# Router of a mixture-of-experts stage: the low parts of the token rows on GpSimd, the first one-hot matrix without the counts, the last tile's statistics over its own columns

## The chip, the cores and the metric

One Trainium2 chip, one of its cores. The time is that of the device, in microseconds, from the first to the last instruction of the program and what lies around it; of several executions the median is given. Everything is float32; products with large weights are made of three matmuls of values rounded for a faster matmul form (high by high, low by high, high by low).

## The reference

256 tokens (and 16 meta tokens) of width 1024 go through a first block (two layers with four gated feed-forward parts, a chunked linear attention and a sliding-window attention) and then a second one, whose end is where the change lies:

```python
mixed = (sigmoid(gate_a) * y_a + sigmoid(gate_b) * y_b) @ w_out
x = layer_norm(DN_ALPHA * h + mixed, ln1_g, ln1_b)
# hier_moe: 4 groups of 8 experts, hidden 512, top 2 of the chosen group
grp = argmax(x @ w_group + b_group)
top_v, top_i = top_k(e_logits of that group, 2)
weights = softmax(top_v) * p_grp
expert = grp * 8 + top_i                     # 512 assignments
order = argsort(expert); rows of x sorted by expert, each expert's rows padded to a block
y[token] += ((silu(gate) * up) @ w_down[e]) * w   for each block
x = layer_norm(DN_ALPHA * x + y, ln2_g, ln2_b)
```

## The kernel before, in words

The program is written engine by engine, with semaphores set by hand; no scheduler reorders it. Until about 1297 us of the profiled execution it works on dense layers. Then comes `wo`, the last projection (eight tiles of 128 features by 256 tokens, two tiles to a weight unit): VectorE (DVE) adds each tile to `h` (line 2188), and TensorE (PE) turns the tile into token rows (`tokens(m)`, a transposition into the banks `xtok` and a product with the 36 routing columns). `bn_stats` over the token rows (lines 2186 and 2191) gives mean and variance of the layer norm, and ScalarE (ACT) then writes the scaled rows twice, once rounded (`m_xhi`, line 1530) and once as they are (`m_o`, line 1532), four pieces of 128x512, and after each it raises the bank's `evac`.

The router runs on DVE, on 128 partitions of tokens (two halves of 128 tokens, side by side): the best group, the best two experts (`first_max`, line 2223), one-hot marks `o1` and `o2`, and their sum `M0, M1` with `m_ready` (line 2242). PE counts with them: `cnt` is how many assignments each expert has, `pos` the place of each token in its expert (columns 0 to 63) and the same plus 64 times the expert (columns 64 to 127). Tokens are put into blocks of 64 slots; the first 32 blocks are the first 64 rows of each expert, and what an expert has beyond 64 rows goes to further blocks, for which the counts must be summed over the experts (lines 2262 to 2268). From that comes `dest`, and from `dest` the one-hot matrix `m_P` of a quad of four blocks (`choose`, `choose_2`), with which PE gathers the rows: `gather(q, n)`, sixteen matmuls for each half (q = 0, 1 and q = 2, 3), with the rounded rows and with their low parts `m_xlo`, which `rows_low` makes (line 2251, 128x512 each, four of them; the semaphore `rows_lo` counts them).

Then the experts run, four to a quad, nine quads here: `expert(quad, s)` multiplies the 64 gathered rows with 2048 KB pieces of weights, two of `w_gate_up` and one of `w_down`. SyncE's queue (SPq) loads the pieces (line 504) into seven places, and each load waits until PE has begun the piece after the one that it overwrites (`exp_begun`). The first pieces land while the router runs.

To keep PE active it multiplies with zeros while it waits: eight matmuls of 512 columns before `m_ready` (four of them clear the output banks), three after `pos`. GpSimd (POOL) issues a few DMAs, and from the first expert's `silu_made` on it makes `x2` (lines 588 and 590, 128x1024 each), which PE needs in the third expert.

## Time and profile before

| | us |
|---|---|
| median of 3 executions (1826.84 to 1829.95) | 1828.28 |
| the profiled execution | 1824.51 |
| its span, first to last instruction | 1822.7 |
| PE busy in it | 1760.8 (97%) |
| DVE, ACT, POOL busy | 1079.8, 709.8, 21.2 |
| HBM read in it | 405.87 MB |

The profiled execution lies 3.8 us under the median. Times in rows are us from the start of the span. PE's busy share counts the multiplications with zeros too, so it doesn't say what bounds a stretch.

### The profile page before, as it was taken

Reading aid. Unit: us, or ns where it says so; the run is one execution under the profiler, and the core shown is the slowest. Engines: PE = TensorE matmul, PEld = TensorE weight load, DVE = VectorE, ACT = ScalarE, POOL = GpSimd, SP = SyncE. Lnnn points to the kernel's source line nnn. Section 1 sums busy time; section 2 is a strip of 40 time slices with the busy share of each in tenths; the row PEclk is TensorE's granted clock in tenths of the full one; section 3 lists DMA queues with packets and bytes.
Section 4 is the critical chain, followed back from the end, with each engine's and each line's share of the span. In section 5 each row is a group of like instructions: output and inputs, shape, how many; then the busy total and the mean of one; then the engine's idle time right before and its main releaser. Section 6 shows DMA issues by size and latency. Waiting matters only on the chain.

```text
span 1822.7 us, 32010 instructions
## 1 busy us (share of the span) xinstructions
PE 1760.8 (97%) x12588; PEld 1427.8 (78%) x12588; DVE 1079.8 (59%) x1923; ACT 709.8 (39%) x1127; POOL 21.2 (1%) x26
## 2 busy tenths in 40 slices
PE   9999999999999999998999999997999999999996
PEld 8999989889999999997899999996953333333332
DVE  6775566687755877668787657867762222222223
ACT  5444453454344544455644446854321101110111
POOL 0000000000000000000000001000020000000000
PEclk9999999999999999999999999998999999999999
DMA  5545333345453355541255545442859999999995
GB/s 232 184 166 207 112 139 139 38 160 177 168 212 135 139 184 193 194 145 47 93 184 184 200 172 184 155 149 89 347 215 415 419 427 429 427 428 428 427 428 215
DMA packets 42337, 409.67 MB, mean 225 GB/s; under 512 B 5304, under 2 KB 5304, under 8 KB 7056
## 3 DMA queue, kind: packets, MB, share of 16 engines
q1 hardware_dynamic: 40032, 402.21, 56.9%
q0 software_dynamic: 1936, 5.79, 1.5%
q8 instruction: 60, 0.98, 0.2%
q10 hardware_dynamic: 288, 0.52, 0.1%
q14 instruction: 21, 0.17, 0.0%
HBM read 405.87 MB, written 2.63 MB: 224 GB/s over the span
## 4 chain that ended last, share of the span: by engine, by line
PE 81%; DVE 10%; DMA 6%; ACT 1%; issue 1%; DVEq 0%; SPq 0%; ACTq 0%
PE ps L596 79%; DMA late<-w_gate_up 6%; PE ps L600 2%; DVE w_lo L1611 1%; DVE h L1717 1%; DVE x_lo L1673 1%; DVE h L1721 1%; DVE rs L1653 1%; DMA raw<-w_units 1%; DVE arena L1975 1%; DVE arena L1895 0%; DVE small L1981 0%; DVE arena L2003 0%; DVE arena L2123 0%; ACT w_hi L1227 0%
## 5 line engine op out<-in xcount | busy, mean ns | idle before, releaser
L596 PE MATMUL ps<-x_hi,w_hi 128*128 128x256 f32 (+1 forms) x2144 | 619.7, 289 | 12.7 <-DVE x_lo L1671 4.5
L596 PE MATMUL ps<-x_lo,w_hi 128*128 128x256 f32 (+1 forms) x2144 | 613.5, 286 | 0.0
L596 PE MATMUL ps<-x_hi,w_lo 128*128 128x256 f32 (+1 forms) x2144 | 611.9, 285 | 0.0
L1611 DVE TENSOR_TENSOR w_lo<-raw,w_hi 128x1024 fp32r<-128x1024 f32 (+1 forms) x352 | 441.2, 1292 | 76.9 <-ACT w_hi L1227 76.6
L596 PEld LDWEIGHTS ps<-x_hi,w_hi 128*128 128x128 f32 x2144 | 407.1, 190 | 23.5 <-issue 9.5
L1227 ACT ACTIVATE w_hi<-raw 128x1024 fp32r<-128x1024 f32 (+1 forms) x352 | 379.5, 1111 | 111.0 <-PE ps L596 86.0
L596 PEld LDWEIGHTS ps<-x_hi,w_lo 128*128 128x128 f32 x2144 | 408.8, 191 | 0.0
L596 PEld LDWEIGHTS ps<-x_lo,w_hi 128*128 128x128 f32 x2144 | 408.0, 190 | 0.2
L596 PE MATMUL ps<-hid_hi,w_hi 128*128 128x272 f32 (+1 forms) x720 | 206.0, 286 | 0.7 <-DVE hid_lo L1673 0.3
L596 PE MATMUL ps<-hid_hi,w_lo 128*128 128x272 f32 (+1 forms) x720 | 204.6, 284 | 0.0
L596 PE MATMUL ps<-hid_lo,w_hi 128*128 128x272 f32 (+1 forms) x720 | 204.0, 283 | 0.0
L1560 ACT ACTIVATE vs<-ps 128x256 f32<-128x256 f32 x32 | 12.3, 384 | 358.3 <-PE ps L596 358.3
L1317 ACT ACTIVATE sg<-sg 128x272 f32<-128x272 f32 (+1 forms) x88 | 37.4, 425 | 278.6 <-DVE sg L1737 278.6
L596 PEld LDWEIGHTS ps<-hid_hi,w_hi 128*128 128x128 f32 x720 | 135.3, 188 | 2.3 <-DVE hid_lo L1673 1.5
L596 PEld LDWEIGHTS ps<-hid_lo,w_hi 128*128 128x128 f32 x720 | 135.9, 189 | 0.1
L596 PEld LDWEIGHTS ps<-hid_hi,w_lo 128*128 128x128 f32 x720 | 135.2, 188 | 0.0
L596 PE MATMUL ps<-soon,moe 128*64 128x512 f32 x528 | 124.8, 614 | 5.7 <-DMA soon<-w_gate_up 5.7
L2371 DVE TENSOR_TENSOR vs<-ps,vs 128x256 f32<-128x256 f32 x32 | 13.6, 425 | 189.3 <-ACT vs L1560 189.3
L596 PE MATMUL ps<-late,moe 128*64 128x512 f32 x496 | 117.3, 613 | 4.6 <-DMA late<-w_gate_up 4.5
L2385 DVE TENSOR_SCALAR x_hi<-ps,moe 128x512 fp32r<-128x512 f32 x32 | 24.0, 751 | 147.9 <-PE ps L596 147.9
L596 PEld LDWEIGHTS ps<-soon,moe 128*64 128x64 f32 x528 | 36.9, 135 | 88.3 <-issue 80.5
L596 PEld LDWEIGHTS ps<-late,moe 128*64 128x64 f32 x496 | 34.6, 135 | 83.1 <-issue 72.7
(328 smaller groups left out, 1990.4 us busy)
## 6 DMA issues: line engine op xcount, KB each, us to landing
raw<-w_units SPq DMA_DIRECT2D x144, 1024.0 KB, 4.8
soon<-w_gate_up SPq DMA_DIRECT2D x33, 2048.0 KB, 20.0
late<-w_gate_up SPq DMA_DIRECT2D x31, 2048.0 KB, 18.3
raw<-w_out_units SPq DMA_DIRECT2D x32, 1408.0 KB, 6.0
soon<-w_down SPq DMA_DIRECT2D x16, 2048.0 KB, 20.4
late<-w_down SPq DMA_DIRECT2D x16, 2048.0 KB, 19.7
bias_rows<-kT POOLq DMA_DIRECT2D x1, 1536.0 KB, 33.4
cst<-table SPq DMA_DIRECT2D x1, 1448.0 KB, 11.9
```

Source lines behind the costliest of these rows:

```text
L596: return nc.tensor.matmul(out_ap, lhsT, rhs, start=start, stop=stop, skip_group_check=True)
L600: return nc.tensor.transpose(out_ap, in_ap, C("ident", 0, k, slice(0, k)))
L1227: nc.scalar.activation(part(w_hi, c, 0, n), raw_slot(u, j * n, n), ACT.Copy).then_inc(hi_made, 1)
L1317: nc.scalar.activation(tile(sg, j, w), tile(sg, j, w), ACT.Silu).then_inc(gate_silu, 1)
L1611: v.tensor_tensor(part(w_lo, c, 0, n), raw_slot(u, j * n, n), part(w_hi, c, 0, n).bitcast(F32), ALU.subtract).then_inc(lo_made, 1)
L1653: then(v.reciprocal(rs[:, 0:w], (var if n % 2 else std)[:, 0:w]))
L1673: e = v.scalar_tensor_tensor(tile(dst[1], m, w), src, factor, hi, ALU.mult, ALU.subtract)
L1717: e = v.tensor_tensor(tile(h, m, w), tile(h, m, w), var[:, 0:w], ALU.mult)
L1721: v.tensor_tensor(tile(h, m - 1, w), tile(h, m - 1, w), tile(zg, m - 1, w), ALU.add)\
L1975: e = v.scalar_tensor_tensor(pb[:, b * row + c:b * row + c + w], bank[:, c:c + w], 0.125, mask, ALU.mult, ALU.add)
L2371: v.tensor_tensor(m_h.rearrange("p (k f) -> p k f", k=2), ps[5][:, 256:512].rearrange("p (f k) -> p k f", k=2), m_sg.rearrange("p (k f) -> ...
L2385: v.tensor_scalar(m_y[0], ps[7][:, :], m_w[:, 0:1], None, ALU.mult).then_inc(yhi_made, 1)
```

## The change

Four edits, all around the router.

1. The four subtractions of `rows_low` leave DVE; GpSimd makes them, each as soon as ACT has written its 128x512 piece.
2. The first quad's one-hot matrix no longer waits for the counts. `pos` gets the same 128 columns with five matmuls in place of eight, ahead of `cnt`. A place of 64 or more pushes the destination out of reach (`FAR`), and what is left, `first`, serves `choose` and `choose_2` of the first quad. The chain over the counts and the real `dest` come behind them. ACT copies `cnt` out of its bank.
3. `tokens(6)` moves from behind the last tile of `wo` into it, ahead of its last two of eight steps. The last tile's `bn_stats` (512 columns for each half of the tokens) is split: 384 columns once tile 6 is turned (`late_turned`), 128 when tile 7 is. Each half then has three sets of sums in place of two.
4. `within` is an existing argument of `project`; `stats_of` names the places of the sums.

```diff
@@ -288,11 +288,12 @@
+        FAR = float(2 * MAXB * SLOTS)
...
@@ -580,6 +582,16 @@
+            for half in range(2):
+                for p in range(2):
+                    t = plan["xtok"].at(2 * p + half)
+                    pool.wait_ge(evac[t[0]], t[1] + 1)
+                    c = half * 512
+                    a = p * D + c
+                    nc.gpsimd.tensor_tensor(m_xlo[p][:, c:c + 512].rearrange("p (k f) -> p k f", k=4),
+                                            m_o[:, a:a + 512].rearrange("p (f k) -> p k f", k=4),
+                                            m_xhi[p][:, c:c + 512].bitcast(F32).rearrange("p (k f) -> p k f", k=4),
+                                            ALU.subtract).then_inc(rows_lo, 1)
...
@@ -1046,6 +1058,8 @@
                     x = turn(ps[x_tiles[p][0]][:, m % 4 * P:(m % 4 + 1) * P], xs)
                     if m % 4 == 3:
                         x.then_inc(full[x_tiles[p][0]], 1)
+                    if m == 6:
+                        x.then_inc(late_turned, 1)
...
@@ -1060,10 +1074,11 @@
 
             for j in range(4):
                 project(u0 + j, T, 2 * j, X, SEQ, x_base=None if j else 88,
-                        between=(lambda: tokens_2(2)) if j == 3 else None)
+                        between=(lambda: tokens_2(2)) if j == 3 else None,
+                        within=(lambda: tokens(6)) if j == 3 else None)
                 if 1 <= j < 3:
                     tokens_2(j - 1)
-            tokens_2(3)
+            tokens(7)
...
@@ -1075,23 +1090,19 @@
             for _ in range(4):
                 mm(ps[0][:, :], m_zero, cst[:, 0:512], False, False)
             pe.wait_ge(m_ready, 1)
+            M0, both = m_r[:, 0:32], m_r[:, 0:64]
+            t = plan["pos"].at(0)
+            bank = free(t)
+            experts = C("iota", 0, 32, slice(0, 1)).rearrange("p (a n) -> p a n", a=1).to_broadcast([1, 2, 32])
+            for at in (0, 64):
+                mm(bank[:, at:at + 64], C("upper"), both, True, False)
+                m = mm(bank[:, at + 32:at + 64], C("ones"), M0, False, at == 0)
+            mm(bank[:, 64:128].rearrange("p (a n) -> p a n", a=2), C("iota", SLOTS, SLOTS + 1, slice(0, 1)).to_broadcast([1, P]),
+               experts, False, True).then_inc(full[t[0]], 1)
             t = plan["cnt"].at(0)
             bank = free(t)
-            M0, M1 = m_r[:, 0:32], m_r[:, 32:64]
             mm(bank[:, 0:32], C("ones"), M0, True, False)
-            mm(bank[:, 0:32], C("ones"), M1, False, True).then_inc(full[t[0]], 1)
-            t = plan["pos"].at(0)
-            bank = free(t)
-            mm(bank[:, 0:32], C("upper"), M0, True, True)
-            mm(bank[:, 32:64], C("upper"), M1, True, False)
-            mm(bank[:, 32:64], C("ones"), M0, False, True)
-            for p, left in enumerate(((("upper", M0),), (("upper", M1), ("ones", M0)))):
-                at = slice(64 + 32 * p, 96 + 32 * p)
-                for i, (name, M) in enumerate(left):
-                    mm(bank[:, at], C(name), M, i == 0, False)
-                m = mm(bank[:, at], C("iota", SLOTS, SLOTS + 1, slice(0, 1)).to_broadcast([1, P]), C("iota", 0, 32, slice(0, 1)),
-                       False, True)
-            m.then_inc(full[t[0]], 1)
+            mm(bank[:, 0:32], C("ones"), m_r[:, 32:64], False, True).then_inc(full[t[0]], 1)
...
@@ -1535,6 +1546,8 @@
             nc.scalar.activation(r_["ge"], r_["ge"], ACT.Exp).then_inc(route_exp, 1)
             act.wait_ge(route_in, 2)
             nc.scalar.activation(r_["ev"], r_["ev"], ACT.Exp).then_inc(route_exp, 1)
+            t = plan["cnt"].at(0)
+            nc.scalar.activation(r_["cnt"], filled(t)[:, 0:32], ACT.Copy).then_inc(evac[t[0]], 1)
...
-            did(v.tensor_scalar(r_["e64"], C("iota", 0, 32), 1.0, float(SLOTS), ALU.add, ALU.mult))
+            did(v.tensor_scalar(r_["e64"], C("iota", 0, 32), float(SLOTS), FAR + SLOTS, ALU.mult, ALU.add))
...
             for i in range(KT):
                 split_to(plan["wo"][0] + i // 2 + 1)
                 if i == 6:
                     for p in range(2):
-                        v.bn_stats(small[:, LN_STATS + 12 * p:LN_STATS + 12 * p + 6], filled(plan["xtok"].at(2 * p))[:, :])
+                        v.bn_stats(stats_of(p, 0), filled(plan["xtok"].at(2 * p))[:, :])
+                if i == 7:
+                    dve.wait_ge(late_turned, 2)
+                    for p in range(2):
+                        v.bn_stats(stats_of(p, 1), ps[plan["xtok"].at(2 * p + 1)[0]][:, 0:384])
                 t = plan["wo"][1].at(i)
                 v.scalar_tensor_tensor(tile(h, i, SEQ), tile(h, i, SEQ), ALPHA, filled(t)[:, 0:SEQ], ALU.mult, ALU.add)\
                     .then_inc(evac[t[0]], 1)
             for p in range(2):
-                last = v.bn_stats(small[:, LN_STATS + 12 * p + 6:LN_STATS + 12 * p + 12],
-                                  filled(plan["xtok"].at(2 * p + 1))[:, :])
-            then(last)
+                last = did(v.bn_stats(stats_of(p, 2), filled(plan["xtok"].at(2 * p + 1))[:, 384:512]))
+            own()
             for p in range(2):
-                last = v.bn_aggr(small[:, LN_MV + 2 * p:LN_MV + 2 * p + 2], small[:, LN_STATS + 12 * p:LN_STATS + 12 * p + 12])
+                last = v.bn_aggr(small[:, LN_MV + 2 * p:LN_MV + 2 * p + 2], stats_of(p, 0, 3))
             last.then_inc(stats_made, 1)
...
@@ -2242,56 +2263,34 @@
             v.tensor_tensor(m_r[:, 0:64], r_["o1"], r_["o2"], ALU.add).then_inc(m_ready, 1)
             v.tensor_tensor(r_["ev"], r_["top2"], r_["top1"], ALU.subtract).then_inc(route_in, 1)
 
-            def rows_low(half):
...
-            rows_low(0)
-            t = plan["cnt"].at(0)
-            per = SEQ // SLOTS
-            over = r_["cmp"][:, 0:32 * per].rearrange("p (e j) -> p e j", j=per)
-            cnt = filled(t)[:, 0:32].rearrange("p (e j) -> p e j", j=1).to_broadcast([P, 32, per])
-            steps = C("iota", 0, per).rearrange("p (e j) -> p e j", e=1).to_broadcast([P, 32, per])
-            v.scalar_tensor_tensor(over, steps, float(SLOTS), cnt, ALU.mult, ALU.is_lt).then_inc(evac[t[0]], 1)
-            mine(t)
-            then(v.tensor_reduce(r_["nb"], over, AX, ALU.add))
-            then(v.tensor_scalar(r_["nb"], r_["nb"], -1.0, 0.0, ALU.add, ALU.max))
-            then(v.tensor_tensor_scan(r_["end"], C("ones", 0, 32), r_["nb"], float(NE), ALU.mult, ALU.add))
-            then(v.tensor_tensor(r_["beg"], r_["end"], r_["nb"], ALU.subtract))
-            then(v.scalar_tensor_tensor(r_["beg"], r_["beg"], float(SLOTS), r_["e64"], ALU.mult, ALU.subtract))
+            def destinations(dst):
+
+                for one, tmp in (("o1", "tmp"), ("o2", "tmp2")):
+                    did(v.tensor_tensor(r_[tmp], r_["em"], r_[one], ALU.mult))
+                own()
+                for k, tmp in enumerate(("tmp", "tmp2")):
+                    did(v.tensor_reduce(r_[dst][:, 2 * k:2 * k + 2], two(r_[tmp]), AX, ALU.add))
+                own()
+
             t = plan["pos"].at(0)
             bank = filled(t)
-            then(v.scalar_tensor_tensor(two(r_["em"]), two(bank[:, 0:64]), float(SLOTS),
-                                        r_["beg"].rearrange("p (a n) -> p a n", a=1).to_broadcast([P, 2, 32]),
-                                        ALU.is_ge, ALU.mult))
-            v.tensor_tensor(two(r_["em"]), two(r_["em"]), two(bank[:, 64:128]), ALU.add).then_inc(evac[t[0]], 1)
+            then(v.tensor_scalar(r_["over"], bank[:, 0:64], float(SLOTS), None, ALU.is_ge))
+            v.scalar_tensor_tensor(r_["em"], r_["over"], FAR, bank[:, 64:128], ALU.mult, ALU.add).then_inc(evac[t[0]], 1)
             mine(t)
-            for one, tmp in (("o1", "tmp"), ("o2", "tmp2")):
-                did(v.tensor_tensor(r_[tmp], r_["em"], r_[one], ALU.mult))
-            own()
-            for k, tmp in enumerate(("tmp", "tmp2")):
-                did(v.tensor_reduce(r_["dest"][:, 2 * k:2 * k + 2], two(r_[tmp]), AX, ALU.add))
-            own()
+            destinations("first")
 
...
-            def choose_2():
+            def choose_2(dest="dest"):
                 for p in range(2):
-                    e = v.scalar_tensor_tensor(m_P[:, p * QUAD:(p + 1) * QUAD], m_iota, col("dest", 2 + p),
+                    e = v.scalar_tensor_tensor(m_P[:, p * QUAD:(p + 1) * QUAD], m_iota, col(dest, 2 + p),
                                                m_t[p], ALU.is_equal, ALU.add)
...
-            choose().then_inc(parts_made, 1)
+            choose("first").then_inc(parts_made, 1)
             dve.wait_ge(parts_made, 1)
-            choose_2().then_inc(p_made, 1)
+            choose_2("first").then_inc(p_made, 1)
+
...
+            mine(plan["cnt"].at(0))
+            over = r_["cmp"][:, 0:32 * per].rearrange("p (e j) -> p e j", j=per)
+            cnt = r_["cnt"].rearrange("p (e j) -> p e j", j=1).to_broadcast([P, 32, per])
...
+            then(v.scalar_tensor_tensor(over, steps, float(SLOTS), cnt, ALU.mult, ALU.is_lt))
...
+            then(v.scalar_tensor_tensor(r_["beg"], r_["beg"], float(SLOTS), r_["e64"], ALU.mult, ALU.subtract))
+            then(v.tensor_tensor(two(r_["over"]), two(r_["over"]),
+                                 r_["beg"].rearrange("p (a n) -> p a n", a=1).to_broadcast([P, 2, 32]), ALU.mult))
+            then(v.tensor_tensor(r_["em"], r_["em"], r_["over"], ALU.add))
+            destinations("dest")
...
-            rows_low(1)
```

The DVE's rows around the edit, before, in the order of its program, from the end of the router's marks (L2242 is `m_ready`; `par` holds all small router tiles, `m_low` is `m_xlo`, `moe` and `x_lo` the halves of the one-hot matrix):

```order
L2242 TENSOR_TENSOR par<-par 128x64
L2243 TENSOR_TENSOR par<-par 128x2
L2251 TENSOR_TENSOR m_low<-h,x_hi 128x512
L2251 TENSOR_TENSOR m_low<-h,x_lo 128x512
L2262 SCALAR_TENSOR_TENSOR par<-cst,ps 128x128
L2264 TENSOR_REDUCE par<-par 128x32
L2265 TENSOR_SCALAR par<-par 128x32
L2266 SCALAR_TENSOR_TENSOR par<-cst,par 128x32
L2267 TENSOR_TENSOR par<-par 128x32
L2268 SCALAR_TENSOR_TENSOR par<-par 128x32
L2271 SCALAR_TENSOR_TENSOR par<-ps,par 128x64
L2274 TENSOR_TENSOR par<-par,ps 128x64
```

The same place in the changed program (L2263 is `m_ready` there):

```order
L2263 TENSOR_TENSOR par<-par 128x64
L2264 TENSOR_TENSOR par<-par 128x2
L2277 TENSOR_SCALAR par<-ps 128x64
L2278 SCALAR_TENSOR_TENSOR par<-par,ps 128x64
L2269 TENSOR_TENSOR par<-par 128x64 x2
L2272 TENSOR_REDUCE par<-par 128x2 x2
L2288 TENSOR_SCALAR moe<-sq,par 128x256 x2
L2293 SCALAR_TENSOR_TENSOR x_lo<-sq,par,moe 128x256 x2
L2327 SCALAR_TENSOR_TENSOR par<-cst,par 128x128
L2328 TENSOR_REDUCE par<-par 128x32
```

Two subtractions and the chain over the counts (L2262 to L2268) no longer stand between the marks and the one-hot matrix; the chain now follows it. GpSimd's rows before, behind its DMAs (`ISA` is an instruction that reloads GpSimd's library, which the compiler puts ahead of its first arithmetic):

```order
L580 DMA cst<-rows 128x1024
L581 DMA cst<-rows 128x1024
L588 ISA
L588 TENSOR_TENSOR h<-h,zg 128x1024
L590 TENSOR_TENSOR h<-h,zg 128x1024
L588 TENSOR_TENSOR h<-h,zg 128x1024
L590 TENSOR_TENSOR h<-h,zg 128x1024
```

And in the changed program:

```order
L582 DMA cst<-rows 128x1024
L583 DMA cst<-rows 128x1024
L591 ISA
L591 TENSOR_TENSOR m_low<-h,x_hi 128x512
L591 TENSOR_TENSOR m_low<-h,x_lo 128x512
L591 TENSOR_TENSOR m_low<-h,x_hi 128x512
L591 TENSOR_TENSOR m_low<-h,x_lo 128x512
L600 TENSOR_TENSOR h<-h,zg 128x1024
L602 TENSOR_TENSOR h<-h,zg 128x1024
```

The reload and four subtractions have moved ahead of `x2`. PE's rows between its multiplications with zeros, before (`par,cst` are the matmuls with M0 and M1, `cst 128x32` those that add 64 times the expert):

```order
L596 MATMUL ps<-cst,moe 128x512 x8
L596 MATMUL ps<-par,cst 128x32 x6
L596 MATMUL ps<-cst 128x32
L596 MATMUL ps<-par,cst 128x32 x2
L596 MATMUL ps<-cst 128x32
L596 MATMUL ps<-cst,moe 128x512 x3
```

And in the changed program:

```order
L608 MATMUL ps<-cst,moe 128x512 x8
L608 MATMUL ps<-par,cst 128x64
L608 MATMUL ps<-par,cst 128x32
L608 MATMUL ps<-par,cst 128x64
L608 MATMUL ps<-par,cst 128x32
L608 MATMUL ps<-cst 128x64
L608 MATMUL ps<-par,cst 128x32 x2
L608 MATMUL ps<-cst,moe 128x512 x3
```

`pos` is complete after five matmuls where it was complete after ten; the eight and the three matmuls with zeros stand as they did.

## Rows read from the trace of the kernel before

**Rows 1.** Windows: stretch, length, each engine's busy us, PE clock share, DMA share, GB/s.

```profile
1345.00:1350.00 5.00, 5.00 (x30) 2.60 (x30) 4.69 (x22) 3.51 (x6) 0.00 (x0) 1.00 0.00 0
...
1360.00:1365.00 5.00, 5.00 (x26) 1.59 (x24) 1.25 (x2) 0.00 (x0) 4.28 (x2) 1.00 1.00 429
```

**Rows 2.** Timeline of SyncE's queue: issues of weight pieces (start us, us, engine, line).

```profile
1357.15 0.33 SPq L504 DMA_DIRECT2D soon<-w_gate_up  x1
...
1777.30 0.33 SPq L504 DMA_DIRECT2D late<-w_down  x1
```

**Rows 3.** Chain that ended last, in order of time, last quad: start us, us, what.

```profile
1773.62 21.91 DMA late<-w_gate_up
```

**Rows 4.** Timeline of DVE around the router (idle before and its releaser in brackets).

```profile
1328.10 1.30 DVE L2191 BATCH_NORM_STATS2 small<-ps 128x6 f32<-128x512 f32 x2 [0.42 <-PE ps L600]
...
1332.28 0.23 DVE L2238 TENSOR_TENSOR par<-par 128x64 f32<-128x64 f32 x1
...
1335.37 0.23 DVE L2242 TENSOR_TENSOR par<-par 128x64 f32<-128x64 f32 x1
...
1335.58 1.08 DVE L2251 TENSOR_TENSOR m_low<-h,x_hi 128x512 fp32r<-128x512 f32 x1
...
1339.11 0.22 DVE L2271 SCALAR_TENSOR_TENSOR par<-ps,par 128x64 f32<-128x64 f32 x1
...
1341.05 0.88 DVE L2294 SCALAR_TENSOR_TENSOR x_lo<-sq,par,moe 128x256 fp32r<-128x256 f32 x2
```

**Rows 5.** Timeline of ACT: the first and the last of its four writes of rows.

```profile
1331.35 0.77 ACT L1532 ACTIVATE h<-ps,small 128x512 f32<-128x512 f32 x1
...
1335.32 0.81 ACT L1532 ACTIVATE h<-ps,small 128x512 f32<-128x512 f32 x1
```

**Rows 6.** Timeline of PE from the last tiles of `wo` to the first expert.

```profile
1322.92 0.38 PE L600 MATMUL ps<-cst,h 128*128 128x128 f32 x2
...
1323.50 0.41 PE L600 MATMUL ps<-cst,h 128*128 128x128 f32 x2
...
1328.37 7.11 PE L596 MATMUL ps<-cst,moe 128*128 128x512 f32 x16
1335.65 1.52 PE L596 MATMUL ps<-par,cst 128*128 128x32 f32 x12 [0.16 <-DVE par L2242]
...
1338.33 2.84 PE L596 MATMUL ps<-cst,moe 128*128 128x512 f32 x6
...
1344.45 0.39 PE L596 MATMUL ps<-x_lo,x_hi 128*128 128x256 f32 x1 [0.28 <-DVE m_low L2251]
...
1346.57 7.42 PE L596 MATMUL ps<-soon,moe 128*64 128x512 f32 x32
```

**Rows 7.** Timelines of GpSimd, and of DVE beside its first instructions.

```profile
1328.04 0.53 POOL L581 DMA_DIRECT2D cst<-rows  x1
1354.64 2.36 POOL L588 TENSOR_TENSOR h<-h,zg 128x1024 f32<-128x1024 f32 x1 [26.07 <-ACT vs L1560]
1357.08 2.36 POOL L590 TENSOR_TENSOR h<-h,zg 128x1024 f32<-128x1024 f32 x1
1359.40 2.46 POOL L588 TENSOR_TENSOR h<-h,zg 128x1024 f32<-128x1024 f32 x1
...
1355.53 1.50 DVE L2317 TENSOR_SCALAR par<-par 128x4 f32<-128x4 f32 x1
...
1360.53 0.75 DVE L2387 SCALAR_TENSOR_TENSOR x_lo<-ps,moe,x_hi 128x512 fp32r<-128x512 f32 x1
```

**Rows 8.** DVE's line 2313 between 1355 and 1361 us: ns min/median/max, starts.

```profile
L2313 DVE TENSOR_TENSOR moe<-moe,kT x2: 278/1362/2445, 1356.9 to 1357.1; 128x128 f32<-128x128 f32 x2
```

**Rows 9.** PE after another long idle, an earlier stage: timeline row, then windows.

```profile
842.59 2.37 PE L600 MATMUL ps<-cst,arena 128*128 128x128 f32 x10 [3.74 <-DVE arena L2003]
...
844.00:846.00 2.00, 2.00 (x15) 1.42 (x15) 1.83 (x7) 1.27 (x4) 0.00 (x0) 0.50 0.00 0
...
848.00:850.00 2.00, 2.00 (x18) 1.21 (x16) 1.86 (x7) 1.46 (x3) 0.00 (x0) 0.77 0.04 8
```

More of the change, by code:

```diff
@@ L290, in two_blocks @@
                         ("o2", 64), ("gtop", 2), ("top1", 2), ("top2", 2), ("place", 2), ("ev", 2), ("pg", 2),
-                        ("w1", 2), ("w2", 2), ("dest", 4), ("cnt", 32), ("nb", 32), ("end", 32), ("beg", 32),
+                        ("w1", 2), ("w2", 2), ("dest", 4), ("first", 4), ("over", 64), ("cnt", 32), ("nb", 32), ("end", 32), ("beg", 32),
                         ("eb", MAXB - NE), ("e64", 32), ("cmp", (MAXB - NE) * 32)):
@@ L343, in two_blocks @@
             sem(n) for n in ("route_in", "route_exp", "m_ready", "table_ready"))
+        late_turned = sem("late_turned")
         rows_lo, g_full, g_made = sem("rows_lo"), sem("g_full"), sem("g_made")
@@ L2175, in _, with stats_of @@
                 to_x(i, tile(zg, i, SEQ), SEQ)
+            def stats_of(p, part, n=1):
+                at = (LN_STATS, 288)[p] + 6 * part
+                return small[:, at:at + 6 * n]
             did(v.tensor_scalar(m_alpha, C("ident"), ALPHA, None, ALU.mult))
@@ L2243, in _ @@
             v.tensor_tensor(r_["ev"], r_["top2"], r_["top1"], ALU.subtract).then_inc(route_in, 1)
-            def rows_low(half):
-                for p in range(2):
-                    mine(plan["xtok"].at(2 * p + half))
-                    c = half * 512
-                    a = p * D + c
-                    v.tensor_tensor(m_xlo[p][:, c:c + 512].rearrange("p (k f) -> p k f", k=4),
-                                    m_o[:, a:a + 512].rearrange("p (f k) -> p k f", k=4),
-                                    m_xhi[p][:, c:c + 512].bitcast(F32).rearrange("p (k f) -> p k f", k=4),
-                                    ALU.subtract).then_inc(rows_lo, 1)
@@ L2283, in col, with choose @@
             def col(x, i):
                 return r_[x][:, i:i + 1]
[L2286 removed]
+            def choose(dest="dest"):
                 for p in range(2):
[L2289 removed]
+                    e = v.tensor_scalar(m_t[p], m_iota, col(dest, p), None, ALU.is_equal)
                 return e
[L2292 removed]
+            def choose_2(dest="dest"):
                 for p in range(2):
[L2294 removed]
+                    e = v.scalar_tensor_tensor(m_P[:, p * QUAD:(p + 1) * QUAD], m_iota, col(dest, 2 + p),
@@ L2317, in move_on @@
                 return v.tensor_scalar(r_["dest"], r_["dest"], -float(QUAD), None, ALU.add)
-            choose().then_inc(parts_made, 1)
+            choose("first").then_inc(parts_made, 1)
             dve.wait_ge(parts_made, 1)
-            choose_2().then_inc(p_made, 1)
+            choose_2("first").then_inc(p_made, 1)
+            per = SEQ // SLOTS
+            mine(plan["cnt"].at(0))
+            over = r_["cmp"][:, 0:32 * per].rearrange("p (e j) -> p e j", j=per)
+            cnt = r_["cnt"].rearrange("p (e j) -> p e j", j=1).to_broadcast([P, 32, per])
+            steps = C("iota", 0, per).rearrange("p (e j) -> p e j", e=1).to_broadcast([P, 32, per])
+            then(v.scalar_tensor_tensor(over, steps, float(SLOTS), cnt, ALU.mult, ALU.is_lt))
+            then(v.tensor_reduce(r_["nb"], over, AX, ALU.add))
+            then(v.tensor_scalar(r_["nb"], r_["nb"], -1.0, 0.0, ALU.add, ALU.max))
+            then(v.tensor_tensor_scan(r_["end"], C("ones", 0, 32), r_["nb"], float(NE), ALU.mult, ALU.add))
+            then(v.tensor_tensor(r_["beg"], r_["end"], r_["nb"], ALU.subtract))
+            then(v.scalar_tensor_tensor(r_["beg"], r_["beg"], float(SLOTS), r_["e64"], ALU.mult, ALU.subtract))
[3 more added lines that the diff above has]
+            destinations("dest")
             quads = r_["cmp"][0:1, 0:MAXB // 4]
```

2 lines of the change are left out of this document (removed).

## The prediction

> **What bounds the kernel now.** I read the windows first. From 1360 us on, the 16 DMA engines move 429 GB/s, and between 1345 and 1350 us they move nothing [rows 1]: the seven places for weight pieces are full, and PE has not begun an expert. The queue's timeline dates this: the load that starts the stream anew is issued at 1357.15, when PE begins the first expert's second product, and the last one at 1777.30 [rows 2]. In the chain that ended last, the last quad holds 21.91 us in which PE waits for a piece [rows 3]. So behind 1357.15 stands a stream of pieces at full rate, then a tail that hangs on the last one. Whatever moves the start of expert 0 (1346.57 [rows 6]) moves 1357.15, and the end, by the same amount, in both directions. Nothing that PE gains later than that counts. The change touches only what stands ahead of 1346.57.
>
> **The path to 1346.57 now.** DVE ends the statistics at 1328.10 + 1.30 = 1329.40, runs the router's short instructions, and `m_ready` is made by the one at 1335.37 [rows 4]. PE, busy with zeros until then, starts the counting matmuls at 1335.65 after 0.16 idle [rows 6]. DVE meanwhile makes two subtractions of 1.08 (from 1335.58) and the count chain, reaches L2271 at 1339.11 and ends the one-hot matrix at 1341.05 + 0.88 = 1341.93 [rows 4]. PE gathers the first half, waits 0.28 for a subtraction of `rows_low`, and gathers the second half from 1344.45 to 1346.57, 2.1 us [rows 6].
>
> **Part 1, tokens(6) and the statistics.** One `tokens(m)` takes PE 1323.50 - 1322.92 = 0.58 [rows 6]. It used to run while DVE added tile 7; now it delays tile 7, and all behind it, by 0.6. The last `bn_stats` shrink: two of 512 columns took 1.30, 0.65 each [rows 4]; at one column per 1 ns or so (1.08 us per 512 strided ones, 0.22 for 64 [rows 4]) two of 128 columns take about 0.42. The two of 384 columns start when tile 6 is turned, 0.6 to 1 us ahead of tile 7's end, and are hidden there. Statistics: 0.60 later, 0.88 shorter, 0.28 earlier in all; so are ACT's writes and DVE's router. But PE's eight matmuls with zeros come 0.6 later as well: they take 16 x 0.427 = 6.83 (start to start, from 7.11 for sixteen passes [rows 6]) and end at 1328.97 + 6.83 = 1335.80, after an undisturbed `m_ready` at 1335.3. This part gains nothing.
>
> **Part 2, `pos` first and no counts.** Twelve passes of 32 columns took 1.45 start to start, 0.24 a matmul [rows 6]; the new five take about 1.29, `cnt` 0.48, the three matmuls with zeros 3 x 0.853 = 2.56 (from 2.84 for six passes [rows 6]). PE thus needs 4.33 from `m_ready` to the first gather, where it had 1335.65 to 1341.93. DVE needs for the two instructions on `pos`, the destinations and the one-hot matrix what it needed before, 1341.93 - 1339.11 = 2.82 [rows 4]. Undisturbed: `pos` at 1335.80 + 1.36, matrix at 1339.98, PE free at 1340.15, gather 4.0 without a stall, expert 0 at 1344.2. That is 2.4 us sooner. The chain over the counts, moved behind the matrix, lies beside the gather, and ACT's copy of `cnt` beside DVE's work.
>
> **Part 3, the subtractions on GpSimd.** This is where I think the change loses. GpSimd's first arithmetic runs from 1354.64 to 1357.00. A DVE instruction on four columns, begun at 1355.53, lasts 1.50 and ends at 1357.03 [rows 7]. Of the two L2313 then, the first slips through in 278 ns and the second takes 2445, from 1357.14 to 1359.59, while GpSimd's second instruction runs from 1357.08 to 1359.44 [rows 7, 8]. So a DVE instruction whose tiles are in SBUF stands still until GpSimd's instruction is over. L2387, which reads PSUM and one SBUF tile, keeps its 0.75 beside the next one [rows 7]. In that place nobody was waiting for DVE. In the new place everybody is: ACT's first write ends at 1331.35 + 0.77 = 1332.12, the last at 1336.13 [rows 5], each 0.28 sooner now, and from 1332.28 to `m_ready` DVE runs 13 short instructions, 0.26 apart, all on SBUF [rows 4].
>
> How long does a subtraction take GpSimd? Half of 2.36 for half the columns is 1.18 [rows 7], the lower bound. The strided read costs DVE 1.08, 2.1 ns a column [rows 4]; with GpSimd slowed as much as DVE is (0.65 for 512 unstrided columns of `bn_stats`, 1.08 here) it would be 1.18 x 1.66 = 1.95, the upper bound. I take 1.3: GpSimd at 2.3 ns a column is already slower than the strided read. By the rows, one DVE instruction passes between two of GpSimd's, 0.23 each. Four of them: 1331.95 + 4 x 1.3 + 3 x 0.25 = 1337.9. Three of the 13 are done by then; ten more take 2.55: `m_ready` at 1340.45 in place of 1335.60. `m_ready` has no cover here, and PE, free at 1336.1, is idle for 4.4 us.
>
> The Trainium skill weighs a little lighter here: by "SBUF — State Buffer", section "Who interferes with whom", a `tensor_reduce` never contends with GpSimd, while two SBUF inputs or a two-port mode do. The trace has no reduction on SBUF beside GpSimd. By that rule two more instructions pass, and the sum below would be 0.5 smaller.
>
> **The clock.** At 842.59 PE came back after 3.74 us idle, and its clock share was 0.50 in the window at 844 and 0.77 in the window from 848 to 850, though it was busy throughout [rows 9]: 1.2 GHz for about 6.3 us after the return. So the 4.4 idle us will cost clock too. The least is nothing, the most 6.3 / 2 = 3.2 us of work; I take 2.0, since other phases between idle and work would shorten the slow stretch.
>
> **The sum.** PE starts at 1340.5; 4.33 to the gather (DVE's 1.36 + 2.82 lies inside), 2.0 for the clock, 4.0 for the gathers: expert 0 at 1350.8, against 1346.57, +4.3 us. The end follows: 1824.5 + 4.3 = 1828.8 for an execution like the profiled one. That one lies 3.8 under the median, so 1828.3 + 4.3 = 1832.5 as a median. With 1.18 and no clock loss it is +1.8; with 1.95 and the full loss +8. The other GpSimd work (`x2`) keeps its place behind the first `silu_made`.
>
> **The rivals.** (a) *GpSimd and DVE don't hinder each other noticeably*, since these DVE instructions are short and the subtractions small. Then part 2 holds: -2.4, 1825.9. Against it are rows 7 and 8. Chance 0.17. (b) *GpSimd starts late.* The reload now has only the time from 1328.04 + 0.53 + 0.6 = 1329.2 [rows 7] to 1331.9 as cover, where it had 26 us. If it outlasts the marks, so that the first subtraction starts just after an undisturbed `m_ready`, no earlier than 1335.3, two of them hold up the destinations and two the one-hot matrix, which then comes at about 1342.3: expert 0 at 1346.4, no change, 1828.1. Each us past 1340 adds one through `rows_lo`. Rows bound the reload only by 0 and 26 us. Chance 0.10. "GPSIMD Engine Reference" of the Trainium skill, section "Instruction dispatch", gives about 6 us for the first call of a freshly loaded kernel; by that, this rival is the one (1329.2 + 6 is 1335.2), and nothing in this trace shows such a load. (c) *The start of expert 0 is not what the end hangs on*, because the stream has slack that no window shows: 1828.3. The unbroken 429 GB/s speaks against it. Chance 0.05. The forecast keeps 0.68.
>
> **Numbers.** The measurement tells no difference under about 0.2%, 3.7 us. The forecast's own range is +1.8 to +8; of its 0.68, 0.43 lies above 3.7 us, and 0.25 below. (a) gives 0.14 within and 0.03 under -3.7 (2.4 gained, plus the scatter of three executions), (b) 0.06 within, 0.02 slower and 0.02 faster, (c) 0.05 within. Slower 0.45, same 0.50, faster 0.05. To leave out no more than 2 in 10, the range takes in (a) and ends where the forecast is nearly used up: 1825.8 to 1836.
>
> **What would show it.** Right: GpSimd's four subtractions lie between 1332 and 1338, three or four DVE router instructions take over 1 us each and end with them, PE waits for `m_ready` over 3 us with a clock share of 0.5 after it, and the first load behind the gap comes at about 1361. Wrong: DVE's router instructions keep their 0.17 to 0.23, or GpSimd starts after 1335; or the first load has moved and the end has not. The sizes I trust least are the strided subtraction on GpSimd and the clock's part.

## The result and the profile after

Over 20 executions of each on one chip the changed kernel takes 1828.8 us (median, 1824.15 to 1834.7) and the kernel before 1824.7 us (1819.7 to 1829.95). The ratio is 1.0021 with a 95% interval of 1.0011 to 1.0031: the change makes the kernel slower, by 3.8 us, between 2.0 and 5.7. The profiled execution took 1829.28 us with a span of 1827.5, against 1824.51 and 1822.7.

The first reading is DVE's timeline of the kernel after, over the stretch of [rows 4]. L2263 makes `m_ready` here; it was L2242 there.

```profile
1328.12 0.50 DVE L2213 BATCH_NORM_STATS2 small<-ps 128x6 f32<-128x128 f32 x2 [0.42 <-PE ps L612]
...
1331.55 1.53 DVE L2259 TENSOR_TENSOR par<-par 128x64 f32<-128x64 f32 x1
1333.12 0.22 DVE L2246 TENSOR_REDUCE par<-par 128x2 f32<-128x64 f32 x1
1333.37 1.22 DVE L2247 TENSOR_TENSOR par<-par 128x64 f32<-128x64 f32 x1
1334.62 1.45 DVE L2249 SCALAR_TENSOR_TENSOR par<-par,cst 128x64 f32<-128x64 f32 x1
1336.11 0.22 DVE L2250 TENSOR_REDUCE par<-par 128x2 f32<-128x64 f32 x1
1336.37 1.18 DVE L2251 TENSOR_TENSOR par<-par 128x64 f32<-128x64 f32 x1
1337.58 0.23 DVE L2261 SCALAR_TENSOR_TENSOR par<-par 128x64 f32<-128x64 f32 x1
...
1339.13 0.23 DVE L2263 TENSOR_TENSOR par<-par 128x64 f32<-128x64 f32 x1
1341.91 0.22 DVE L2277 TENSOR_SCALAR par<-ps 128x64 f32<-128x64 f32 x1 [2.49 <-PE ps L608]
```

Beside it stands GpSimd's timeline of the same stretch, its four subtractions:

```profile
1331.48 1.53 POOL L591 TENSOR_TENSOR m_low<-h,x_hi 128x512 fp32r<-128x512 f32 x1 [2.88 <-ACT h L1543]
1332.97 1.53 POOL L591 TENSOR_TENSOR m_low<-h,x_lo 128x512 fp32r<-128x512 f32 x1
1334.47 1.52 POOL L591 TENSOR_TENSOR m_low<-h,x_hi 128x512 fp32r<-128x512 f32 x1
1335.96 1.51 POOL L591 TENSOR_TENSOR m_low<-h,x_lo 128x512 fp32r<-128x512 f32 x1
```

Lay one beside the other. DVE's first instruction on 64 columns begins 0.07 us after GpSimd's first and ends with it, at 1333.08 and 1333.01. The third, fourth and sixth end at 1334.59, 1336.07 and 1337.55, each next to an end of GpSimd's (1334.50, 1335.99, 1337.47). They take 1.18 to 1.53 us, where such an instruction took 0.23 [rows 4]. The two reductions on SBUF keep their 0.22 in the middle of a GpSimd instruction. From 1337.58 on, with GpSimd idle, the rest run 0.26 apart.

PE's timeline of the kernel after, over the stretch of [rows 6]:

```profile
1328.40 7.11 PE L608 MATMUL ps<-cst,moe 128*128 128x512 f32 x16
1339.41 1.85 PE L608 MATMUL ps<-par,cst 128*128 128x64 f32 x8 [3.90 <-DVE par L2263]
...
1342.68 4.63 PE L608 MATMUL ps<-cst,moe 128*128 128x512 f32 x6
1346.74 0.68 PE L608 MATMUL ps<-x_lo,x_hi 128*128 128x256 f32 x1
...
1351.07 7.44 PE L608 MATMUL ps<-soon,moe 128*64 128x512 f32 x32
```

And windows of the kernel after, with the columns of [rows 1] (PE's clock share is the third from the end):

```profile
1335.00:1340.00 5.00, 1.10 (x5) 0.59 (x4) 4.12 (x11) 2.10 (x4) 2.47 (x2) 0.95 0.99 421
1340.00:1345.00 5.00, 5.00 (x16) 3.65 (x16) 2.88 (x12) 0.20 (x1) 0.00 (x0) 0.50 0.30 122
1345.00:1350.00 5.00, 5.00 (x28) 3.62 (x27) 4.54 (x22) 1.64 (x4) 0.00 (x0) 0.87 0.00 2
```

The last one again, in a narrower window:

```profile
1346.00:1348.00 2.00, 2.00 (x11) 1.29 (x10) 1.76 (x11) 0.00 (x0) 0.00 (x0) 0.92 0.00 0
```

PE had 0.16 us of idle time ahead of the counting matmuls [rows 6] and now has 3.90. The first window's 0.95 is 0.5 us at a share of 0.50, so from about 1339.5 on, 0.1 us after PE's return, the granted clock share is 0.50, the 1.2 GHz level. It stays there through the second window, in which PE was busy throughout. The share of 0.92 from 1346 to 1348 says when it rose: 0.33 us of these 2 us at 0.50 and the rest at 1.00 give 0.92, so at about 1346.33. Six passes with zeros take 4.63 where they took 2.84 [rows 6]. Expert 0 starts at 1351.07, against 1346.57 [rows 6], 4.50 later.

The queue of weight pieces, in SyncE's timeline of the kernel after, follows:

```profile
1361.67 0.33 SPq L506 DMA_DIRECT2D soon<-w_gate_up  x1
...
1782.03 0.33 SPq L506 DMA_DIRECT2D late<-w_down  x1
```

The first load behind the gap is 4.52 later than in [rows 2], the last 4.73, and the span is 4.8 longer.

### The profile page after: what moved, and what is told of

It reads as the page before. It is cut to its first block, busy times and chain, and to the rows that moved or that the text cites. A ratio compares the mean times of both kernels' runs of the same rounds, so it can differ in the third digit from the quotient of the medians.

```text
span 1827.5 us, 32006 instructions
## 1 busy us (share of the span) xinstructions
PE 1760.9 (96%) x12582; PEld 1425.8 (78%) x12582; DVE 1081.2 (59%) x1927; ACT 710.1 (39%) x1128; POOL 27.2 (1%) x30
## 4 chain that ended last, share of the span: by engine, by line
PE 81%; DVE 10%; DMA 6%; ACT 1%; issue 1%; DVEq 0%; SPq 0%; ACTq 0%
PE ps L608 79%; DMA late<-w_gate_up 6%; PE ps L612 2%; DVE w_lo L1624 1%; DVE h L1730 1%; DVE x_lo L1686 1%; DVE h L1734 1%; DVE rs L1666 1%; DMA raw<-w_units 1%; DVE arena L1988 1%; DVE arena L1908 0%; DVE small L1994 0%; DVE arena L2136 0%; ACT w_hi L1238 0%; DVE arena L2016 0%
```

## The experiments

**How they are compared.** The dense stages ahead of the router vary by some us from one execution to the next, for every kernel. So each trace is counted from the same event: DVE's addition for tile 6 of `wo`, the last one that no edit moves. DVE's timelines of before and of after show it:

```profile
1323.12 0.42 DVE L2188 SCALAR_TENSOR_TENSOR h<-h,ps 128x256 f32<-128x256 f32 x1 [2.11 <-PE ps L596]
```

```profile
1322.49 0.42 DVE L2210 SCALAR_TENSOR_TENSOR h<-h,ps 128x256 f32<-128x256 f32 x1 [2.11 <-PE ps L608]
```

So 0.63 of each instant's difference between these two traces has nothing to do with the change. In the table "expert 0" is its first matmul, counted from there; "first load" is the issue that starts the stream anew. Each kernel was timed in turns with the kernel before on the same chip.

| kernel | expert 0 | against before | first load | against before | first load to end of span | ratio of times (95%) |
|---|---|---|---|---|---|---|
| before | 23.45 | | 34.03 | | 465.55 | |
| after | 28.58 | +5.13 | 39.18 | +5.15 | 465.83 | 1.0021 (1.0011 to 1.0031) |
| e1_rows_on_dve | 21.34 | -2.11 | 43.91 | +9.88 | 465.18 | 1.0074 (1.0052 to 1.0096) |
| e2_gpsimd_alone | 31.04 | +7.59 | 41.61 | +7.58 | 464.05 | 1.0035 (1.0018 to 1.0051) |
| e3_pe_kept_busy | 25.46 | +2.01 | 36.10 | +2.07 | 465.86 | 1.0004 (0.9988 to 1.0020) |
| e4_gpsimd_writes_only | 21.28 | -2.17 | 31.93 | -2.10 | 465.41 | 0.9998 (0.9981 to 1.0014) |
| e5b_gpsimd_after_matrix | 25.93 | +2.48 | 36.51 | +2.48 | 464.96 | 1.0013 (0.9997 to 1.0029) |
| e8_rows_on_dve_x2_later | 21.30 | -2.15 | 31.89 | -2.14 | 465.38 | 0.9985 (0.9973 to 0.9997) |
| e9_no_statistics_x2_later | 21.39 | -2.06 | 31.97 | -2.06 | 465.71 | 0.9986 (0.9972 to 1.0001) |
| e10_x2_later_alone | 23.35 | -0.10 | 33.93 | -0.10 | 464.22 | 0.9992 (0.9980 to 1.0004) |
| e12_seven_zeros | 21.28 | -2.17 | 31.86 | -2.17 | 465.18 | 0.9990 (0.9978 to 1.0002) |

Two things are to be read from it. From the first load to the end it is 464 to 466 us whatever came before, so the stream does carry the start to the end, within the 1.8 us by which these single executions differ. And divided by 1824.7, the shift of the first load lies in the interval of the times for every kernel (after: 5.15, 0.28%; e8: -0.12%), for e1 at its lower end (0.54%, where the interval is 0.52 to 0.96%). The trace's difference up to the first load is the finer instrument; the times agree with it.

**e1: the subtractions back on DVE.** Edits 2 and 3 stay.

```diff
-            for half in range(2):            # GpSimd's loop
-                for p in range(2):
...
+            rows_low(0)
...
+            rows_low(1)
```

`rows_low(0)` stands on DVE behind the marks, `rows_low(1)` and the zeroing of `m_pT[1]` and `m_y` ahead of the chain over the counts.

> The changed kernel with the four subtractions back on VectorE (two right behind m_ready, two behind the first one-hot matrix, and the zeroing of m_pT and m_y ahead of the count chain); edits 2 and 3 stay. Port theory: nothing holds VectorE's marks, m_ready comes about 4.7 us sooner than in the changed kernel, no low clock at the gather, expert 0 about 2.1 us sooner than in the kernel before; time 2 us under before, 6 to 7 under the change. Rival, that the loss comes from the new order of pos, cnt and the matrix (edit 2): expert 0 stays about 4.5 us later than before, time 4 us over before.

Expert 0 came 2.11 us sooner, as expected, and the time was 0.74% longer, which no theory had. The cause stands behind expert 0. PE's timeline of e1, then DVE's and GpSimd's, just after the first products of expert 0:

```profile
1361.05 0.69 PE L602 MATMUL ps<-cst,vs 128*128 128x128 f32 x2 [10.34 <-DVE vs L2390]
```

```profile
1350.26 2.96 DVE L2296 SCALAR_TENSOR_TENSOR x_lo<-sq,par,moe 128x256 fp32r<-128x256 f32 x2
1353.15 2.42 DVE L2303 TENSOR_SCALAR moe<-sq,par 128x256 f32<-128x256 f32 x1
1355.49 2.42 DVE L2305 TENSOR_SCALAR kT<-sq,par 128x256 f32<-128x256 f32 x1
1357.84 2.50 DVE L2303 TENSOR_SCALAR moe<-sq,par 128x256 f32<-128x256 f32 x1
...
1360.58 0.41 DVE L2390 TENSOR_TENSOR vs<-ps,vs 128x256 f32<-128x256 f32 x1
```

```profile
1350.32 2.62 POOL L590 TENSOR_TENSOR h<-h,zg 128x1024 f32<-128x1024 f32 x1 [23.31 <-ACT vs L1563]
...
1357.85 2.34 POOL L592 TENSOR_TENSOR h<-h,zg 128x1024 f32<-128x1024 f32 x1
```

PE stood still for 10.34 us, waiting for the gated product of expert 0 (`vs`, L2390). DVE had its one-hot work for the second quad ahead of that instruction. GpSimd's `x2`, which the first `silu_made` lets go, started 0.06 us into it, and four of DVE's instructions went at GpSimd's pace. In the trace of before the order is the other way round, as DVE's timeline there shows:

```profile
1353.04 0.41 DVE L2303 TENSOR_SCALAR kT<-sq,par 128x256 f32<-128x256 f32 x1
1354.53 0.42 DVE L2371 TENSOR_TENSOR vs<-ps,vs 128x256 f32<-128x256 f32 x1 [1.08 <-ACT vs L1560]
```

DVE is done with the second quad 1.08 us before the gated product can be made, and GpSimd starts at 1354.64 [rows 7], behind it. In e1 expert 0 is 2.11 sooner, and DVE comes to L2296 of the second quad 1.20 later, counted from tile 6 (29.35 against 28.15), so the margin is used up. The six instructions from L2296 on take 2.2 us alone (1358.74 to 1360.92 in e8) and took 10.4 here, so 8.2 us of the stall are the meeting with GpSimd. PE's clock adds to it: the sixteen passes from 1362.82 on take 5.34, where they take 3.65 in the trace of before. DVE is held up by GpSimd here as in the change itself, in a second place, and it hides the gain of edit 2. The trace gives e1 9.88 us at the first load; the times give 0.52 to 0.96%, which is 9.5 to 17.5 us, and what may be more than 9.9 of it is not explained.

**e2: GpSimd's subtractions alone.** The kernel before with edit 1.

```diff
-            rows_low(0)
-            rows_low(1)
+            for half in range(2):            # GpSimd's loop, as in the change
```

> The kernel before with the four subtractions moved to GpSimd and nothing else. Port theory: four or five of VectorE's router instructions take 1.2 to 1.5 us, m_ready comes about 4.7 us later than in the kernel before, TensorE idles 5 us and works at half clock after it; expert 0 about 5.5 us later, time 5 to 6 us over before. Rival, edit 2 is the loss: VectorE is rid of 4 x 1.08 us, expert 0 about 2 us sooner than before.

The loss was larger than expected, +7.59 at expert 0 and 1.0035 in time. PE's timeline of e2, and two of its windows:

```profile
1339.84 2.46 PE L606 MATMUL ps<-par,cst 128*128 128x32 f32 x12 [4.63 <-DVE par L2252]
```

```profile
1348.00:1350.00 2.00, 2.00 (x5) 0.97 (x4) 1.86 (x9) 0.00 (x0) 0.00 (x0) 0.50 0.00 0
1350.00:1352.00 2.00, 2.00 (x17) 2.00 (x16) 1.86 (x8) 0.80 (x2) 0.00 (x0) 0.89 0.00 0
```

After 4.63 idle PE's clock share was 0.50 from 1340.20 to 1350.44 (the 0.89 of the last window is 0.44 us at 0.50), over nearly the whole of the counting part, which is the longer one of before. So edit 1 alone makes more than the whole loss, and edits 2 and 3 take 2.5 of it away in the changed kernel.

**e3: PE kept busy through the wait.** The changed kernel with four more matmuls with zeros ahead of the counting ones; they only fill time.

```diff
-            for _ in range(4):
+            for _ in range(8):
                 mm(ps[0][:, :], m_zero, cst[:, 0:512], False, False)
             pe.wait_ge(m_ready, 1)
```

> The changed kernel with four more multiplications by zero ahead of the wait for m_ready (12 instead of 8, 3.4 us more). VectorE's router is held as before, but TensorE idles under 1 us. If the low clock of 1339.5 to 1346.3 us came from the 3.9 us of idleness, it is gone, and expert 0 starts about 3.0 us sooner than in the changed kernel, 1.5 us later than before the change; time 1 to 2 us over before. Rival, the low clock has another cause: granted clock 0.5 again in some 5 us window after m_ready, expert 0 as late as in the changed kernel or later.

PE's timeline and windows of e3:

```profile
1345.19 1.08 PE L608 MATMUL ps<-par,cst 128*128 128x64 f32 x8 [0.50 <-DVE par L2263]
```

```profile
1346.00:1348.00 2.00, 2.00 (x12) 1.41 (x12) 1.20 (x7) 0.20 (x1) 0.00 (x0) 1.00 0.50 205
```

`m_ready` is as late as in the changed kernel (counting matmuls 16.95 behind the addition of tile 6, 16.92 there), but PE works through the wait, the share stays at 1.00, and the first eight counting passes take 1.08 in place of 1.85. Expert 0 comes 3.12 sooner than in the changed kernel. So the clock's part in the loss is 3.1 us, and the wait's the rest.

**e4: GpSimd writes and doesn't read.** A memset in place of each subtraction, in the same place behind the same wait. The low parts of the rows are left out (zeros).

```diff
-                    nc.gpsimd.tensor_tensor(m_xlo[p][:, c:c + 512]..., ALU.subtract).then_inc(rows_lo, 1)
+                    nc.gpsimd.memset(m_xlo[p][:, c:c + 512].bitcast(F32), 0.0).then_inc(rows_lo, 1)
```

> The changed kernel with a memset of the low parts to zero on GpSimd in place of each subtraction: the same four writes of 128x512, no read; the gathered rows then lack their low parts. If only a GpSimd instruction that reads SBUF holds up VectorE instructions with two SBUF inputs, the router's 0.23 us instructions keep their length, m_ready comes where edits 2 and 3 alone would put it, and expert 0 starts about 2.4 us sooner than in the kernel before. If any GpSimd instruction holds them up, each tensor_tensor that meets a memset ends with it, and m_ready is late by most of the four memsets' time (each perhaps 0.5 to 1.2 us).

GpSimd's timeline of e4, and DVE's beside its first two instructions:

```profile
1331.12 0.53 POOL L591 MEMSET m_low<- 128x512 f32 x1 [2.86 <-ACT h L1540]
1332.46 0.53 POOL L591 MEMSET m_low<- 128x512 f32 x1 [0.81 <-ACT h L1540]
```

```profile
1331.22 0.23 DVE L2256 TENSOR_TENSOR par<-par 128x64 f32<-128x64 f32 x1
...
1332.51 0.22 DVE L2248 TENSOR_TENSOR par<-par 128x64 f32<-128x64 f32 x1
```

Both DVE instructions lie inside a memset and keep their 0.22 to 0.23, and so do the other eleven up to the marks. So it isn't GpSimd being active, nor its writing to SBUF, that holds DVE up. It is the subtraction, which differs in that it reads two tiles of SBUF and lasts longer; the two weren't separated. With the hold-up gone, expert 0 is 2.17 sooner than before: nearly the 2.4 that edit 2 was worth in the prediction's part 2. (This kernel has no subtractions at all, so it shows where the loss comes from and is no kernel to use.) The time, 0.9998, doesn't show it, but its interval takes in the -0.12% that 2.1 us would be.

**e8, e9, e10: `x2` later.** In all three GpSimd's `x2` waits until DVE has copied out expert 0's second product, and DVE's work for the second quad comes behind expert 0's gated product (`m_h`) in place of ahead of it. The first of the two moves:

```diff
-            pool.wait_ge(silu_made, 1)
+            pool.wait_ge(evac[7], E_BASE[7] + 1)
```

e8 is e1 with it, e9 is e8 without edit 3, e10 is the kernel before with it.

> e1 with two moves: GpSimd's x2 instructions wait until VectorE has finished expert 0, and VectorE makes the next quad's one-hot matrix behind expert 0's product instead of ahead of it. Theory from e1: expert 0 started 2.1 us sooner there than in the kernel before (counted from VectorE's add of tile 6), but VectorE's preparation of the second quad then met x2 on GpSimd and was held 2.4 us for each of four instructions, so that the first product of expert 0 came 10 us late. Without that meeting both the start of expert 0 and the first load behind the gap come about 2.1 us sooner than in the kernel before; time 2 us under it (0.1%, little more than the interval). Rival, that the 10 us have another cause (a semaphore order of edit 2): TensorE idles about 10 us after expert 0's first matmuls again.

> e8 without edit 3 (tokens(6) and the statistics as in the kernel before). If edit 3 gains nothing, as predicted, because the multiplications with zeros end 0.6 us later too, then the time from the add of tile 6 to expert 0 is within 0.3 us of e8's. If the statistics' 0.28 us come through, e8 is 0.3 us shorter; if tokens(6) inside tile 7 costs its 0.6 us, e9 is shorter by that.

> The kernel before with the two moves of e8 alone. VectorE was ready 1.1 us ahead of expert 0's silu there, so that nothing on the path changes: start of expert 0 and first load behind the gap within 0.3 us of the kernel before; same time. It says that a gain of e8 comes from the router and not from these moves. Rival: the moves themselves gain or lose over 1 us.

GpSimd's, DVE's and PE's timelines of e8:

```profile
1363.99 2.41 POOL L590 TENSOR_TENSOR h<-h,zg 128x1024 f32<-128x1024 f32 x1 [30.06 <-DVE x_lo L2406]
```

```profile
1339.98 0.23 DVE L2253 TENSOR_TENSOR par<-par 128x64 f32<-128x64 f32 x1
1340.20 1.09 DVE L2262 TENSOR_TENSOR m_low<-h,x_hi 128x512 fp32r<-128x512 f32 x1
...
1342.16 0.22 DVE L2280 TENSOR_SCALAR par<-ps 128x64 f32<-128x64 f32 x1
```

```profile
1340.68 0.97 PE L598 MATMUL ps<-par,cst 128*128 128x64 f32 x8
```

`x2` now starts when DVE is done with the second quad, PE's 10.34 us of idle time is gone, and the 2.1 us reach the first load and the end: 0.9985 (0.9973 to 0.9997), 2.7 us less than before by that ratio. It is the one kernel here that is faster than both with its whole interval, but by little: e9 and e12, which the traces put within 0.1 us of it, end at 1.0001 and 1.0002. The traces show this gain better than the times. The move of `x2` by itself is worth 0.1 us (e10), so the gain is edit 2's (with `rows_low(1)` and the zeroing ahead of the count chain, as in e1). Edit 3 is worth 0.09 us at expert 0 (e8 against e9), nothing that a time could show.

**e5b: the same subtractions on GpSimd, in another place.** The changed kernel with `pool.wait_ge(p_made, 1)` ahead of GpSimd's loop, and `x2` later as in e8. GpSimd starts when the first quad's one-hot matrix is done.

> The changed kernel with GpSimd's four subtractions held back until the first one-hot matrix is made, and the two moves of e8. Port theory: the router's marks and the matrix keep their 0.2 us instructions, TensorE keeps its clock, but the gather now waits for 2 x 1.5 us of GpSimd and then 2 x 1.5 again, and VectorE's count chain and zeroing behind the matrix are held instead; expert 0 about 2 to 3 us later than in the kernel before, 2 to 3 us sooner than in the changed kernel. Rival, that GpSimd's subtractions are the loss by their length wherever they stand: as late as the changed kernel, 5 us.

GpSimd's and PE's timelines of e5b:

```profile
1345.36 1.51 POOL L592 TENSOR_TENSOR m_low<-h,x_hi 128x512 fp32r<-128x512 f32 x1 [11.04 <-DVE x_lo L2294]
1346.84 1.50 POOL L592 TENSOR_TENSOR m_low<-h,x_lo 128x512 fp32r<-128x512 f32 x1
```

```profile
1348.48 0.55 PE L609 MATMUL ps<-x_lo,x_hi 128*128 128x256 f32 x1 [2.85 <-POOL m_low L592]
```

One of its windows:

```profile
1350.00:1352.00 2.00, 2.00 (x12) 2.00 (x12) 1.90 (x4) 1.02 (x2) 1.34 (x1) 0.54 0.02 4
```

Nothing on DVE's way to the matrix is held up. Now the first gather waits 2.85 us for the second subtraction, and the clock falls again behind it (a share of 0.54 from 1350 to 1352), which the expectation had excluded. It costs 2.48 where the changed kernel costs 5.13: the place of GpSimd's work counts, and of the two places that were tried neither was free.

**e12: one matmul with zeros fewer.** e8 with `range(3)` in place of `range(4)` ahead of `m_ready`.

> Rows on VectorE, x2 later (as in e8_rows_on_dve_x2_later), and TensorE makes seven of its matmuls with zeros ahead of the counting matmuls in place of eight. In e8 the counting matmuls began 0.47 us after the marks were ready, because TensorE was still at its zeros. Theory (the zeros hide what edit 3 gains for the statistics): the counting matmuls begin 0.1 to 0.2 us after the marks, expert 0's first matmul comes about 0.3 us sooner, 21.0 us behind VectorE's add of tile 6 where e8 had 21.30, and the time is about 0.15 to 0.17% under the kernel before, no more than 0.02% better than e8. Rival (the zeros do more than fill time: they keep the clock up): the clock falls to 0.5 after a short idle time, and expert 0 comes later than in e8.

DVE's timeline of e12, and PE's:

```profile
1336.42 0.23 DVE L2253 TENSOR_TENSOR par<-par 128x64 f32<-128x64 f32 x1
...
1338.60 0.22 DVE L2280 TENSOR_SCALAR par<-ps 128x64 f32<-128x64 f32 x1
```

```profile
1336.70 1.08 PE L598 MATMUL ps<-par,cst 128*128 128x64 f32 x8 [0.27 <-DVE par L2253]
```

The counting matmuls begin 0.05 us after `m_ready` (1336.65), where it was 0.47 in e8 (1340.21 to 1340.68). Expert 0 gained 0.02 us, not 0.3: the expectation missed, and its rival too, since the clock held. L2280, the first instruction on `pos`, stands 2.18 us behind `m_ready` both times (1342.16 - 1339.98, 1338.60 - 1336.42), because DVE makes two subtractions in between. The zeros did keep PE 0.42 longer in e8, but nothing waited for it. The ratio, 0.9990 (0.9978 to 1.0002), is that of e8 within the intervals.

## Why the prediction was right, and where it was wrong

**The mechanism was right.** GpSimd's four subtractions lie between 1331.48 and 1337.47, DVE's two-input instructions end with them, PE waits for `m_ready` and works at half the clock behind the wait, expert 0 and the end follow. The signs that the prediction named came: four router instructions of over 1 us, a wait of over 3 us (3.90), and the first load behind the gap at about 1361 (1361.67). The forecast of +4.3 us compares with 4.50 at expert 0 in the two profiles, 5.13 counted from tile 6, and 3.8 (2.0 to 5.7) in the times. e2 shows that edit 1 alone makes the loss; e4 and e8 that without it edit 2 gains.

**What failed is the step "Numbers".** The chances gave 0.50 to a difference within 0.2% and 0.45 to slower. Two faults made this. First, a quarter of all chance was the forecast's own part below 3.7 us. A forecast of +4.3 next to a bound of 3.7 can't say on which side it falls, and the bound itself was too wide: 20 executions of each tell 0.1% apart (1.0011 to 1.0031), not 0.2%. The measured 3.8 us lies clear of zero, and only 0.1 above that bound. Second, the rivals (a), (b) and (c) held 0.32 together, 0.25 of it within the bound, and none of them happened. (a) had [rows 7] and [rows 8] directly against it, in which a DVE instruction of this kind stands still beside GpSimd; 0.17 was too much for it. The likeliest mechanism said slower, and the sum over the cases hid that.

**The base.** 1832.5 stands 3.7 above the measured 1828.8. Of that, 3.6 is the base: the median of three executions was 1828.28, that of 20 is 1824.7. The difference was good to 0.5 us, well inside what the times can tell. The profiled execution's own 1824.51 lies nearer to 1824.7, but by luck: single executions of the kernel before went from 1819.7 to 1829.95.

**The terms, one by one.** The profiled execution after is 0.63 us earlier at tile 6, which has to be taken off the prediction's instants.
- *A subtraction on GpSimd*: 1.3 taken, bounds 1.18 and 1.95; it is 1.51 to 1.53. That is 1.29 times the lower bound; the upper bound took 1.66, from a strided subtraction and an unstrided `bn_stats` of DVE, two different instructions.
- *Who passes*: three of DVE's 13 instructions done by the end of the subtractions, ten behind them, `m_ready` at 1340.45. In fact six were done and seven came behind: both reductions ran through, and a fourth held-up instruction ended with the fourth subtraction. GpSimd made no room for the ones between either, its four follow each other 1.49 to 1.50 apart; `m_ready` ended at 1339.36, with the 0.63 added 1339.99, 0.46 better. The rule of the Trainium skill, "SBUF — State Buffer", section "Who interferes with whom", by which a reduction never contends with GpSimd, would have made the sum 0.5 smaller, and the trace agrees with it (0.22 us at 1333.12 and at 1336.11). The idle time was 3.90 where 4.4 was forecast.
- *The clock*: 2.0 taken of a bound of 3.2. From PE's return to the first gather it is 1346.74 - 1339.41 = 7.33 in place of 4.33, so 3.0; e3 gives 3.1. The hope that other phases would shorten the slow stretch was wrong: it lasted 6.8 us, to 1346.33.
- *The gathers and the sum*: the gathers took 1351.07 - 1346.74 = 4.33 in place of 4.0. The start of PE was 0.46 better than forecast, the clock 1.0 worse, the gathers 0.33 worse, so the sum was about 0.9 short: +5.13 from tile 6, not +4.3. It looks right beside the 4.50 of the two profiles because the profiled execution of after came to tile 6 0.63 sooner, and that is chance.
- *Part 2*: 2.4 sooner, undisturbed. e4 gives 2.17, e8 2.15.
- *Part 1*: the delay of tile 7 was 0.66 (0.6), the last `bn_stats` 0.50 in place of 1.30 (0.42), and their sums over three sets took 0.33 in place of 0.28. Together 0.09 sooner, not 0.28, and e8 against e9 shows that 0.09 at expert 0. "This part gains nothing" holds. Its reason, PE's zeros, does not hold with the subtractions on DVE: e12 takes one of them away and nothing comes sooner. In the changed kernel itself that reason was never reached, since `m_ready` was late. In e4, where nothing holds DVE, it does hold: the marks are ready at 1334.55, the counting matmuls start at 1335.02, and DVE waits 1.78 for `pos`.

**The rivals.** (a), no hindrance: refuted by the 1.53 in place of 0.23. (b), a late GpSimd: the first subtraction begins at 1331.48, 0.09 after ACT's write is done. The reload had the 2.88 us before it as cover and needed no more. The 6 us that the Trainium skill gives for a first call ("GPSIMD Engine Reference", section "Instruction dispatch") do not show here; why not, no run here tells. (c), slack in the stream: refuted, 464 to 466 us from the first load to the end in each kernel. What no rival named is the meeting of DVE and GpSimd behind expert 0 (e1). It was in reach: [rows 7] show DVE held up by `x2` in the trace of before right behind the work for the second quad. The prediction looked at that place as evidence and not as a place that would move.

**What stays open.** e1 differs from e8 in GpSimd's wait and in the order of DVE's work for the second quad together; which of the two alone would suffice wasn't run. That the margin of 1.08 us was used up is read from the traces, not tried by itself. What it is in GpSimd's subtraction that holds DVE up, its reads or its length, isn't shown either (e4). And each position in the table is that of one execution.
